# Prompt attention of a hybrid decoder step: heads in pairs, and block products in place of a running sum

## The chip, the cores and the metric

The kernel runs on one core of one Trainium2 chip. The metric is the time of one execution on the device in microseconds (us). The engines have short names in the profile: PE (matrix multiply) with its weight loads PEld, DVE (vector), ACT (activation), POOL (GpSimd) and SP (which feeds the DMA queues). PSUM, the memory that PE writes, is the tile `ps` of eight banks with 512 fp32 columns each.

## The reference

One step of a decoder trunk of four layers for 512 prompt tokens and 8 x 8 sample tokens, width 1024. Layer 1 mixes tokens by stick-breaking attention with 16 heads of 64. For the prompt, this is all that the change touches:

```
qkv = (u @ w_qkv).reshape(Bn, T, 3, N_HEADS, HEAD_DIM)
...
z = jnp.einsum('bqhd,bkhd->bhqk', q_blk, keys).astype(jnp.float32) * (HEAD_DIM ** -0.5)
z = z + bias.astype(jnp.float32)[None, :, None, None]
mask = k_pos[None, :] < q_pos[:, None]
log_stay = jnp.where(mask, jax.nn.log_sigmoid(-z), 0.0)
between = lax.cumsum(log_stay, axis=3, reverse=True) - log_stay
a = jnp.where(mask, jnp.exp(jax.nn.log_sigmoid(z) + between), 0.0)
return jnp.einsum('bhqk,bkhd->bqhd', a.astype(vals.dtype), vals)
```

So each key's weight needs the sum of softplus(z) over all later keys that the query may see. Softplus is computed as max(z, 0) + ln(1 + exp(-|z|)).

## The kernel before

Only the stage called `attention` matters here. It lies after the products with `w_qkv` and some transposes, and before the attention of the sample tokens, which starts when it has ended. Scores are held with keys on the 128 partitions and queries along the columns. One head has four **pieces**, one for each block of 128 keys, taken from the last block (`kb` = 3) to the first: the piece of block `kb` has `512 - 128 kb` columns, so the pieces of a head have 128, 256, 384 and 512 columns, 1280 together. There are 16 heads and 64 pieces. All of it is fp32.

For one piece the engines do this, each in its own loop, tied together by semaphores:

- PE, `scores` (L715): the product of keys and queries, over the 64 rows of that head, into one of four banks. It waits until `weights` of four pieces earlier has read that bank.
- DVE, `biased`: adds the head's bias into `ZB` (L1762), then takes |z| into `EX` (L1764). ACT, `soft`: exp (L1293) and ln (L1295) of `EX`. DVE, `softplus`: max and add into `SP` (L1773).
- POOL, `mask_sp`: zeroes the part of the diagonal block that no query may see (L2198), copies it into `SUM` (L2203) and adds the earlier pieces' sum to the rest (L2205).
- PE, `cumulate`: adds onto the scores the product of a negated triangle with `SP` (L723) and, but for a head's first piece, of negated ones with the previous `SUM` (L727). Two pieces behind `scores`.
- ACT, `weights`: exp with the bias, from the bank into `AT` (L1303). POOL, `mask_a`: zeroes the diagonal block of that (L2215).
- PE, `values` (L740), once in a head, after its four pieces: four products with `VT`, 64 output rows. DVE, `take` (L1779), once in two heads: copies the result out of its bank.

A fp32 matmul has two records in the trace, one for each of its two passes over the columns, each with a weight load; so 64 calls of `scores` are 128 records. No queue or planner orders the work: each engine works its own loop off in order. PE's is the following.

```
for k in range(4 * NH + 5):
    if k < 4 * NH:
        scores(k)
    if 2 <= k < 4 * NH + 2:
        cumulate(k - 2)
    if k % 4 == 0 and 8 <= k:
        values(k // 4 - 2)
```

## Time and profile before

| what | us |
|---|---|
| median of 3 runs (lowest, highest) | 3921.86 (3911.35, 3925.43) |
| the profiled execution, its own time | 3924.92 |
| its span, from the first to the last instruction | 3923.2 |
| prompt attention, from DVE's first read of scores to the last copy out of PSUM | 999 to 1213.1 |
| mean granted PE clock over the whole span | 0.932 of 2.4 GHz |

The trace's times count from the first instruction of the span. A granted clock of 1.00 is 2.4 GHz and 0.50 is 1.2 GHz; a number in between is a mean over a stretch with both. A record's duration holds the time that its result takes to arrive, so consecutive matmuls overlap in their records: what a matmul costs PE is the distance from its start to the next one's start.

### The profile page before, as it was taken

Reading aid. Unit: us, or ns where it says so; the run is one execution under the profiler, and the core shown is the slowest. Engines: PE = TensorE matmul, PEld = TensorE weight load, DVE = VectorE, ACT = ScalarE, POOL = GpSimd, SP = SyncE. Lnnn points to the kernel's source line nnn. Section 1 sums busy time; section 2 is a strip of 40 time slices with the busy share of each in tenths; the row PEclk is TensorE's granted clock in tenths of the full one; section 3 lists DMA queues with packets and bytes.
Section 4 is the critical chain, followed back from the end, with each engine's and each line's share of the span. In section 5 each row is a group of like instructions: output and inputs, shape, how many; then the busy total and the mean of one; then the engine's idle time right before and its main releaser. Section 6 shows DMA issues by size and latency. Waiting matters only on the chain.

```text
span 3923.2 us, 76827 instructions
## 1 busy us (share of the span) xinstructions
PE 3539.9 (90%) x33232; PEld 3231.5 (82%) x33232; DVE 1576.9 (40%) x2263; ACT 1298.6 (33%) x2088; POOL 410.5 (10%) x862
## 2 busy tenths in 40 slices
PE   5998999989788789999688789988999989999996
PEld 3997999979336579999578678867999979889996
DVE  1435443231451244442534654454444244354422
ACT  2223443222442234442333322323444222244422
POOL 1000000000452100000000432300000000000000
PEclk9999999999797599999888799989999999989998
DMA  4554223353102242224432100014222444222221
GB/s 158 151 153 152 80 81 107 94 172 92 49 1 86 87 132 86 80 83 118 138 92 61 39 17 15 20 42 132 86 80 83 118 145 114 79 59 81 83 79 46
DMA packets 450251, 350.04 MB, mean 89 GB/s; under 512 B 14652, under 2 KB 417100, under 8 KB 449596
## 3 DMA queue, kind: packets, MB, share of 16 engines
q1 hardware_dynamic: 439776, 308.58, 26.6%
q0 software_dynamic: 9616, 35.34, 2.8%
q8 instruction: 208, 3.41, 0.4%
q10 hardware_dynamic: 608, 2.36, 0.2%
q14 instruction: 43, 0.35, 0.0%
HBM read 333.44 MB, written 12.79 MB: 88 GB/s over the span
## 4 chain that ended last, share of the span: by engine, by line
PE 83%; DVE 8%; issue 3%; POOL 2%; ACT 2%; DMA 2%; POOLq 0%; DVEq 0%; ACTq 0%
PE ps L593 58%; PE ps L891 6%; PE ps L817 3%; PE ps L818 2%; PE ps L819 2%; PE ps L659 2%; DMA raw<-in_ada_w 1%; PE ps L688 1%; PE ps L740 1%; PE ps L778 1%; DVE XMf L1838 1%; PE ps L604 1%; DVE XMl L1842 1%; PE ps L770 1%; PE ps L723 1%
## 5 line engine op out<-in xcount | busy, mean ns | idle before, releaser
L1590 DVE TENSOR_TENSOR SL<-raw,SH 128x1024 fp32r<-128x1024 f32 x408 | 500.5, 1227 | 1544.4 <-ACT SH L1205 1544.4
L1205 ACT ACTIVATE SH<-raw 128x1024 fp32r<-128x1024 f32 x408 | 432.2, 1060 | 1596.3 <-PE ps L593 1358.4
L593 PE MATMUL ps<-Uh,SH 128*128 128x288 f32 x3744 | 806.1, 297 | 1.5 <-DVE GP L2069 1.1
L593 PE MATMUL ps<-Uh,SL 128*128 128x288 f32 x3744 | 801.7, 296 | 0.0
L593 PE MATMUL ps<-Ul,SH 128*128 128x288 f32 x3744 | 801.0, 296 | 0.0
L593 PEld LDWEIGHTS ps<-Uh,SH 128*128 128x128 f32 x3744 | 602.4, 189 | 18.4 <-issue 16.9
L593 PEld LDWEIGHTS ps<-Uh,SL 128*128 128x128 f32 x3744 | 603.3, 189 | 0.0
L593 PEld LDWEIGHTS ps<-Ul,SH 128*128 128x128 f32 x3744 | 603.3, 189 | 0.0
L593 PE MATMUL ps<-Hh,SH 128*128 128x288 f32 x1792 | 390.7, 300 | 2.4 <-DVE Hl L1829 2.4
L593 PE MATMUL ps<-Hh,SL 128*128 128x288 f32 x1792 | 383.9, 296 | 0.0
L593 PE MATMUL ps<-Hl,SH 128*128 128x288 f32 x1792 | 383.7, 296 | 0.0
L593 PEld LDWEIGHTS ps<-Hh,SH 128*128 128x128 f32 x1792 | 287.7, 189 | 13.1 <-issue 12.5
L593 PEld LDWEIGHTS ps<-Hh,SL 128*128 128x128 f32 x1792 | 288.9, 189 | 0.0
L593 PEld LDWEIGHTS ps<-Hl,SH 128*128 128x128 f32 x1792 | 288.9, 189 | 0.0
L2162 POOL COPY TL<-GP 128x2 f32 (+1 forms) x104 | 45.5, 438 | 1425.4 <-ACT GP L1205 1065.6
L817 PE MATMUL ps<-XMh,SH 128*128 128x288 f32 x448 | 141.5, 316 | 36.8 <-DVE XMl L1842 36.8
L659 PE MATMUL ps<-raw,CT 128*32 128x256 f32 x1408 | 120.3, 428 | 42.6 <-DMA raw<-in_ada_w 42.4
L1742 DVE SCALAR_TENSOR_TENSOR CV<-GP,ST,CV 128x592 f32<-128x592 f32 x176 | 147.0, 835 | 25.6 <-DVE CV L1742 0.6
L818 PE MATMUL ps<-XMl,SH 128*128 128x288 f32 x448 | 137.1, 306 | 0.0
L819 PE MATMUL ps<-XMh,SL 128*128 128x288 f32 x448 | 136.3, 304 | 0.0
L1205 ACT ACTIVATE Hh<-Hf (+1 forms) x112 | 76.0, 685 | 170.4 <-DVE Hf L2102 108.2
L817 PEld LDWEIGHTS ps<-XMh,SH 128*128 128x128 f32 x448 | 89.0, 199 | 45.8 <-issue 36.3
(407 smaller groups left out, 4854.3 us busy)
## 6 DMA issues: line engine op xcount, KB each, us to landing
raw<-in_ada_w SPq DMA_DIRECT2D x176, 512.0 KB, 4.3
raw<-in_f_w_gu SPq DMA_DIRECT2D x176, 512.0 KB, 3.8
raw<-in_f_w_down SPq DMA_DIRECT2D x64, 448.0 KB, 3.8
raw<-in_a_w_in SPq DMA_DIRECT2D x48, 512.0 KB, 5.1
raw<-in_f_w_down SPq DMA_DIRECT2D x32, 512.0 KB, 4.1
raw<-in_b_w_qkv SPq DMA_DIRECT2D x24, 512.0 KB, 4.6
raw<-in_r_w_rkv SPq DMA_DIRECT2D x24, 512.0 KB, 4.2
PRE<-in_ada_w SPq DMA_DIRECT2D x4, 2048.0 KB, 25.4
```

The costliest lines, as they stand in the source:

```text
L593: mm = pe.matmul(ps[:, b + h, 0:TH], w, a[:, k, h * TH:(h + 1) * TH], start=on, stop=off)
L604: mm = pe.matmul(ps[32 * g:32 * g + 32, SS, 0:TQ], ones[:], SQ[:, n % 2, g * TQ:(g + 1) * TQ], start=(k == 0), stop=(k == KT - 1), skip_gr ...
L659: mm = pe.matmul(ps[32 * g:32 * g + 32, ADA, 0:2 * P], CT[:, k, :], src[:, 2 * P * g:2 * P * g + 2 * P], start=(k == 0), stop=(k == KT - 1 ...
L688: mm = pe.transpose(ps[0:cols, bank, g * width:g * width + rows], a, ident[0:rows, 0:rows])
L817: pe.matmul(out, wh, hi[:, cols], start=start, stop=False)
L818: pe.matmul(out, wh, lo[:, cols], start=False, stop=False)
L819: return pe.matmul(out, wl, hi[:, cols], start=False, stop=stop)
L891: mm = lambda out, l, r, start=False: pe.matmul(out, l, r, start=start, stop=True, skip_group_check=True)
L1205: copy = lambda out, in_: act.activation(out, in_, ACT.Copy)
L1590: dve.tensor_tensor(SL[:, m.mod(2)], raw[:, n.mod(4)], SH[:, m.mod(2)].bitcast(F32), ALU.subtract)\
L1742: ins = dve.scalar_tensor_tensor(CV[:, 0:CW], src, w(tap), CV[:, 0:CW], ALU.mult, ALU.add)
L2162: pool.tensor_copy(tl[:, 0:HIST], GP[:, g, NP_TOK:NP_TOK + HIST])
```

## The change

- Heads are taken in pairs that lie in the two halves of the partitions. A piece is now both heads of a pair: 8 pairs, 32 pieces. DVE's, ACT's and POOL's instructions on `ZB`, `EX` and the masks cover both heads at once; `weights` stays one instruction for each head, with its own bias.
- `scores` issues the two heads' products one behind the other, the one on rows 0 to 63 and the other on rows 64 to 127, into two banks. There are three such pairs of banks in place of four single ones; the wait is for `weights` of three pieces earlier. `values` alternates between the heads, whose outputs are partitions 0 to 63 and 64 to 127 of one bank.
- `SUM`, its copy and its addition on POOL are gone. In their place `later_blocks` multiplies the negated ones with each of the earlier pieces' softplus tiles, which all stay in `SPS`: for the second, third and fourth piece 1, 2 and 3 products a head, with 128, 128 + 256 and 128 + 256 + 384 columns. It waits for `biased` of its own piece.
- The order on PE is `later_blocks(k)`, `scores(k + 2)`, `cumulate(k)`; `values` follows the first piece of the next pair. On POOL `mask_a(k - 1)` now stands ahead of `mask_sp(k)`. On ACT `weights` is two pieces behind `soft`, not three.

```
@@ -174,11 +174,22 @@
         KR = sb("KR", [P, 4, D], F32, u_at + 20 * D)
         KS = sb("KS", [NS_TOK, D], F32, h_at + 19 * S // 4)
         w1_at, w2_at, w3_at = u_at + 20 * D, h_at + 2 * S, h_at + 19 * S // 4
-        ZB = sb("ZB", [P, 2, 512], F32, w1_at)
-        EX = sb("EX", [P, 2, 512], F32, w1_at + 4096)
-        SP = sb("SP", [P, 2, 512], F32, w1_at + 8192)
-        SUM = sb("SUM", [P, 2, 512], F32, w1_at + 12288)
-        AT = sb("AT", [P, 2, 1280], F32, w2_at)
+        ZB = sb("ZB", [P, 2, 2, 512], F32, w1_at)
+        EX = sb("EX", [P, 2, 2, 512], F32, w1_at + 8192)
+        AT = sb("AT", [P, 2, 2, 1280], F32, h_at + 15 * S // 4)
+        SPS = [sb(f"SP{q}", [P, 2, 1280], F32, at) for q, at in enumerate((h_at + 15 * S // 4 + 20480, w2_at))]
+        PIECES = 4 * KT
+
+        def block_cols(pc):
+
+
+            return pc // 4, 3 - pc % 4, NP_TOK - (3 - pc % 4) * P, (0, P, 3 * P, 6 * P)[pc % 4]
+
+        def spent(pc):
+
+            p, kb, w, at = block_cols(pc)
+            return SPS[p % 2][:, :, at:at + w]
+
...
@@ -704,50 +715,56 @@
                 pe.wait_ge(tr_free, count["tr"])
 
 
-                def where(pc):
-                    return pc // 4, 3 - pc % 4
-
                 def scores(pc):
-                    h, kb = where(pc)
-                    r, w = 64 * (h % 2), NP_TOK - kb * P
-                    if due(pc - 3):
-                        pe.wait_ge(a_ready, pc - 3)
-                    pe.matmul(ps[:, pc % 4, 0:w], KF[r:r + HD, h // 2, kb * P:(kb + 1) * P],
-                              QF[r:r + HD, h // 2, kb * P:NP_TOK], start=True, stop=True).then_inc(z_ready, 1)
+                    p, kb, w, _ = block_cols(pc)
+                    if due(pc - 2):
+                        pe.wait_ge(a_ready, pc - 2)
+                    for h, hh in HEADS:
+                        mm = pe.matmul(ps[:, 2 * (pc % 3) + h, 0:w], KF[hh, p, kb * P:(kb + 1) * P], QF[hh, p, kb * P:NP_TOK],
+                                       start=True, stop=True)
+                    mm.then_inc(z_ready, 1)
 
                 def cumulate(pc):
 
-                    h, kb = where(pc)
-                    w = NP_TOK - kb * P
+                    p, kb, w, _ = block_cols(pc)
                     pe.wait_ge(spm_ready, pc + 1)
-                    mm = pe.matmul(ps[:, pc % 4, 0:w], ntri[:], SP[:, pc % 2, 0:w], start=False, stop=True,
-                                   skip_group_check=True)
-                    if kb < 3:
-                        pe.wait_ge(sum_ready, pc)
-                        mm = pe.matmul(ps[:, pc % 4, P:w], nones[:], SUM[:, (pc - 1) % 2, 0:w - P],
-                                       start=False, stop=True, skip_group_check=True)
+                    for h in range(2):
+                        mm = pe.matmul(ps[:, 2 * (pc % 3) + h, 0:w], ntri[:], spent(pc)[:, h], start=False, stop=True,
+                                       skip_group_check=True)
                     mm.then_inc(cum_done, 1)
 
-                def values(h):
-                    r, b = 64 * (h % 2), 4 + h // 2 % 2
-                    pe.wait_ge(am_ready, 4 * h + 4)
-                    if due(h // 2 - 1):
-                        pe.wait_ge(av_read, h // 2 - 1)
-                    at = AT[:, h % 2, :]
+                def later_blocks(pc):
+
+                    p, kb, w, _ = block_cols(pc)
+                    if kb == 3:
+                        return
+                    pe.wait_ge(zb_ready, pc + 1)
+                    for h in range(2):
+                        for later in range(3 - kb, 0, -1):
+                            pe.matmul(ps[:, 2 * (pc % 3) + h, later * P:w], nones[:], spent(pc - later)[:, h], start=False,
+                                      stop=True, skip_group_check=True)
+
+                def values(p):
+                    pe.wait_ge(am_ready, 4 * p + 4)
+                    if due(p - 1):
+                        pe.wait_ge(av_read, p - 1)
                     for kb in range(4):
-                        o0 = (0, P, 3 * P, 6 * P)[3 - kb]
-                        w = NP_TOK - kb * P
-                        mm = pe.matmul(ps[r:r + HD, b, kb * P:NP_TOK], VT[:, kb, h * HD:(h + 1) * HD],
-                                       at[:, o0:o0 + w], start=(kb == 0), stop=(kb == 3))
+                        _, _, w, at = block_cols(3 - kb)
+                        for h, hh in HEADS:
+                            mm = pe.matmul(ps[hh, 6 + p % 2, kb * P:NP_TOK], VT[:, kb, (2 * p + h) * HD:(2 * p + h + 1) * HD],
+                                           AT[:, p % 2, h, at:at + w], start=(kb == 0), stop=(kb == 3), skip_group_check=True)
                     mm.then_inc(av_done, 1)
 
-                for k in range(4 * NH + 5):
-                    if k < 4 * NH:
-                        scores(k)
-                    if 2 <= k < 4 * NH + 2:
-                        cumulate(k - 2)
-                    if k % 4 == 0 and 8 <= k:
-                        values(k // 4 - 2)
+                for k in range(2):
+                    scores(k)
+                for k in range(PIECES + 1):
+                    if k < PIECES:
+                        later_blocks(k)
+                        if k + 2 < PIECES:
+                            scores(k + 2)
+                        cumulate(k)
+                    if k % 4 == 0 and 4 <= k:
+                        values(k // 4 - 1)
 
 
                 pe.wait_ge(av_read, KT + 2)
@@ -1287,27 +1304,28 @@
 
                 def soft(pc):
 
-                    w = NP_TOK - (3 - pc % 4) * P
-                    e = EX[:, pc % 2, 0:w]
+                    _, _, w, _ = block_cols(pc)
+                    e = EX[:, pc % 2, :, 0:w]
                     act.wait_ge(abs_ready, pc + 1)
                     act.activation(e, e, ACT.Exp, scale=-1.0).then_inc(act_seq, 1)
                     act.wait_ge(act_seq, pc + 1)
                     act.activation(e, e, ACT.Ln, bias=1.0).then_inc(ln_ready, 1)
 
                 def weights(pc):
-                    h, kb = pc // 4, 3 - pc % 4
-                    w, o0 = NP_TOK - kb * P, (0, P, 3 * P, 6 * P)[3 - kb]
+                    p, _, w, at = block_cols(pc)
                     act.wait_ge(cum_done, pc + 1)
-                    if due(h - 1):
-                        act.wait_ge(av_done, h - 1)
-                    act.activation(AT[:, h % 2, o0:o0 + w], ps[:, pc % 4, 0:w], ACT.Exp, bias=BB[:, h:h + 1])\
-                       .then_inc(a_ready, 1)
+                    if due(p - 1):
+                        act.wait_ge(av_done, p - 1)
+                    for h in range(2):
+                        ins = act.activation(AT[:, p % 2, h, at:at + w], ps[:, 2 * (pc % 3) + h, 0:w], ACT.Exp,
+                                             bias=BB[:, 2 * p + h:2 * p + h + 1])
+                    ins.then_inc(a_ready, 1)
 
                 act.preload_act_table_set("natural_log_exp_and_others")
-                for k in range(4 * NH + 3):
-                    if k >= 3:
-                        weights(k - 3)
-                    if k < 4 * NH:
+                for k in range(PIECES + 2):
+                    if k >= 2:
+                        weights(k - 2)
+                    if k < PIECES:
                         soft(k)
 
                 for g in range(4 * NB):
@@ -1755,40 +1773,39 @@
                 dve.wait_ge(kv_out, 64)
 
                 def biased(pc):
-                    h, kb = pc // 4, 3 - pc % 4
-                    w = NP_TOK - kb * P
-                    z, e = ZB[:, pc % 2, 0:w], EX[:, pc % 2, 0:w]
+                    p, _, w, _ = block_cols(pc)
+                    z, e = ZB[:, pc % 2, :, 0:w], EX[:, pc % 2, :, 0:w]
                     dve.wait_ge(z_ready, pc + 1)
-                    dve.tensor_scalar(z, ps[:, pc % 4, 0:w], BB[:, h:h + 1], None, ALU.add).then_inc(zb_ready, 1)
+                    dve.tensor_tensor(z, ps[:, 2 * (pc % 3):2 * (pc % 3) + 2, 0:w],
+                                      BB[:, 2 * p:2 * p + 2].rearrange("p (h o) -> p h o", o=1).broadcast_to([P, 2, w]), ALU.add)\
+                       .then_inc(zb_ready, 1)
                     dve.wait_ge(zb_ready, pc + 1)
                     dve.scalar_tensor_tensor(e, z, -1.0, z, ALU.mult, ALU.max).then_inc(abs_ready, 1)
 
                 def softplus(pc):
-                    w = NP_TOK - (3 - pc % 4) * P
+                    p, _, w, _ = block_cols(pc)
                     dve.wait_ge(ln_ready, pc + 1)
-                    if due(pc - 1):
-                        dve.wait_ge(cum_done, pc - 1)
-                    if due(pc - 1):
-                        dve.wait_ge(sum_ready, pc - 1)
-                    dve.scalar_tensor_tensor(SP[:, pc % 2, 0:w], ZB[:, pc % 2, 0:w], 0.0, EX[:, pc % 2, 0:w],
+                    if due(p - 1):
+                        dve.wait_ge(cum_done, 4 * (p - 1))
+                    dve.scalar_tensor_tensor(spent(pc), ZB[:, pc % 2, :, 0:w], 0.0, EX[:, pc % 2, :, 0:w],
                                              ALU.max, ALU.add).then_inc(sp_ready, 1)
 
                 def take(p):
 
-                    dve.wait_ge(av_done, 2 * p + 2)
-                    dve.tensor_copy(Hf[:, p, 0:NP_TOK], ps[:, 4 + p % 2, :]).then_inc(av_read, 1)
-
-                for k in range(4 * NH + 10):
-                    if k < 4 * NH:
+                    dve.wait_ge(av_done, p + 1)
+                    dve.tensor_copy(Hf[:, p, 0:NP_TOK], ps[:, 6 + p % 2, :]).then_inc(av_read, 1)
+
+                for k in range(PIECES + 4):
+                    if k < PIECES:
                         if due(k - 1):
                             dve.wait_ge(sp_ready, k - 1)
                         biased(k)
-                    if 1 <= k < 4 * NH + 1:
+                    if 1 <= k < PIECES + 1:
                         softplus(k - 1)
-                    if k % 8 == 5 and k >= 13:
-                        take(k // 8 - 1)
-
-                dve.wait_ge(cum_done, 4 * NH)
+                    if k % 4 == 2 and 6 <= k:
+                        take(k // 4 - 1)
+
+                dve.wait_ge(cum_done, PIECES)
                 dve.memset(QB[:], 0.0).then_inc(av_read, 1)
                 dve.wait_ge(av_read, KT + 1)
                 dve.tensor_copy(QB[0:HD, :, 0, :], QF[0:HD, :, NP_TOK:T])
@@ -2190,36 +2207,25 @@
                     pool.dma_start(PG[:, n % 4, :], cache[0, bass.ds(page[n % (NB * NPAGE)], 1)]
                                    .rearrange("o t h d -> (o t) (h d)")).then_inc(page_full[n % 4], 16)
 
+                def diagonal(a):
+
+                    return pool.affine_select(out=a, in_=a, compare_op=ALU.is_gt, fill=0.0, base=0, pattern=[[0, 2], [1, P]],
+                                              channel_multiplier=-1)
+
                 def mask_sp(pc):
-                    h, kb = pc // 4, 3 - pc % 4
-                    w = NP_TOK - kb * P
                     pool.wait_ge(sp_ready, pc + 1)
-                    d = SP[:, pc % 2, 0:P]
-                    pool.affine_select(out=d, in_=d, compare_op=ALU.is_gt, fill=0.0, base=0, pattern=[[1, P]],
-                                       channel_multiplier=-1).then_inc(spm_ready, 1)
-                    pool.wait_ge(spm_ready, pc + 1)
-                    if due(pc):
-                        pool.wait_ge(cum_done, pc)
-                    ins = pool.tensor_copy(SUM[:, pc % 2, 0:P], d)
-                    if kb < 3:
-                        ins = pool.tensor_tensor(SUM[:, pc % 2, P:w], SUM[:, (pc - 1) % 2, 0:w - P],
-                                                 SP[:, pc % 2, P:w], ALU.add)
-                    ins.then_inc(sum_ready, 1)
-                    pool.wait_ge(sum_ready, pc + 1)
+                    diagonal(spent(pc)[:, :, 0:P]).then_inc(spm_ready, 1)
 
                 def mask_a(pc):
-                    h, kb = pc // 4, 3 - pc % 4
-                    o0 = (0, P, 3 * P, 6 * P)[3 - kb]
+                    p, _, _, at = block_cols(pc)
                     pool.wait_ge(a_ready, pc + 1)
-                    d = AT[:, h % 2, o0:o0 + P]
-                    pool.affine_select(out=d, in_=d, compare_op=ALU.is_gt, fill=0.0, base=0, pattern=[[1, P]],
-                                       channel_multiplier=-1).then_inc(am_ready, 1)
-
-                for k in range(4 * NH + 3):
-                    if k < 4 * NH:
+                    diagonal(AT[:, p % 2, :, at:at + P]).then_inc(am_ready, 1)
+
+                for k in range(PIECES + 1):
+                    if k >= 1:
+                        mask_a(k - 1)
+                    if k < PIECES:
                         mask_sp(k)
-                    if k >= 3:
-                        mask_a(k - 3)
 
                 def same_sequence(a):
 
```

## Rows read from the trace of the kernel before

**Rows 1.** The page: span, and the chain that ended last by engine.
```profile
span 3923.2 us, 76827 instructions
...
PE 83%; DVE 8%; issue 3%; POOL 2%; ACT 2%; DMA 2%; POOLq 0%; DVEq 0%; ACTq 0%
```

**Rows 2.** Stretches: busy us of PE, PEld, DVE, ACT, POOL, then clock, DMA.
```profile
999.00:1025.53 26.53, 21.07 (x37) 9.87 (x37) 13.07 (x26) 10.64 (x24) 9.40 (x24) 0.50 0.00 1
1088.79:1136.86 48.07, 39.82 (x120) 18.57 (x120) 25.75 (x50) 21.10 (x47) 26.36 (x61) 0.97 0.00 1
1136.86:1191.47 54.61, 45.63 (x121) 20.05 (x120) 25.74 (x50) 22.27 (x49) 25.96 (x60) 0.87 0.00 0
999.00:1213.10 214.10, 178.06 (x474) 80.65 (x474) 104.12 (x200) 87.31 (x192) 102.82 (x241) 0.86 0.00 1
```

**Rows 3.** Waits, 1100.7 to 1124.5: total us, times, longest.
```profile
ACT EX L1293 <- DVE EX L1764: 12.5, 6, 4.2
...
PEld ps L723 <- POOL SP L2198: 5.1, 4, 1.4
```

**Rows 4.** Timeline of one head: start, duration, engine, line.
```profile
1100.72 2.37 PE L740 MATMUL ps<-AT,VT 128*64 128x512 f32 x8 [0.73 <-POOL AT L2215]
...
1103.02 0.70 PE L715 MATMUL ps<-QF,KF 64*128 64x256 f32 x2
...
1103.64 1.12 PE L723 MATMUL ps<-SP,ntri 128*128 128x512 f32 x2
...
1104.61 0.81 PE L727 MATMUL ps<-SUM,nones 128*128 128x384 f32 x2
...
1105.35 0.91 PE L715 MATMUL ps<-QF,KF 64*128 64x384 f32 x2
...
1112.65 2.37 PE L740 MATMUL ps<-AT,VT 128*64 128x512 f32 x8 [0.73 <-POOL AT L2215]
```

**Rows 5.** Timeline: first mask, and last copy out of PSUM.
```profile
1003.71 0.28 POOL L2198 TENSOR_SCALAR_AFFINE_SELECT SP<-SP 128x128 f32<-128x128 f32 x1 [11.80 <-issue]
...
1212.39 0.69 DVE L1779 COPY Hf<-ps 128x512 f32<-128x512 f32 x1 [7.82 <-PE ps L740]
```

**Rows 6.** Timeline of PE in a later layer, at 2297.6.
```profile
2297.59 1.91 PE L891 MATMUL ps<-BMs,UWs 64*64 64x512 f32 x8
2299.31 1.05 PE L891 MATMUL ps<-KMs,TMs 64*64 64x512 f32 x4
```

**Rows 7.** Timeline of PE in the transposes.
```profile
987.20 1.15 PE L688 MATMUL ps<-ident,KF 128*128 128x128 f32 x8 [0.19 <-ACT KR L1205]
```

**Rows 8.** Groups of lines, 999 to 1213.1: busy us, mean ns, idle before.
```profile
L2205 POOL TENSOR_TENSOR SUM<-SUM,SP 128x128 f32<-128x128 f32 (+2 forms) x48 | 41.3, 859 | 0.1
...
L1764 DVE SCALAR_TENSOR_TENSOR EX<-ZB 128x128 f32<-128x128 f32 (+1 forms) x64 | 34.5, 538 | 2.2
L1773 DVE SCALAR_TENSOR_TENSOR SP<-ZB,EX 128x128 f32<-128x128 f32 (+1 forms) x64 | 33.8, 529 | 1.8 <-ACT EX L1295 0.8
L1303 ACT ACTIVATE AT<-ps,BB 128x128 f32<-128x128 f32 (+1 forms) x64 | 33.0, 515 | 15.0 <-PE ps L727 11.8 <-PE ps L723 1.9
...
L1293 ACT ACTIVATE EX<-EX 128x128 f32<-128x128 f32 (+1 forms) x64 | 29.9, 467 | 113.6 <-DVE EX L1764 113.6
L2215 POOL TENSOR_SCALAR_AFFINE_SELECT AT<-AT 128x128 f32<-128x128 f32 x64 | 24.6, 386 | 6.9 <-ACT AT L1303 2.5
...
L2203 POOL COPY SUM<-SP 128x128 f32<-128x128 f32 x64 | 20.4, 318 | 10.1 <-PE ps L727 7.1 <-PE ps L723 0.3
...
L2198 POOL TENSOR_SCALAR_AFFINE_SELECT SP<-SP 128x128 f32<-128x128 f32 x64 | 18.9, 295 | 98.1 <-DVE SP L1773 86.2 <-issue 11.8
```

**Rows 9.** Groups by shape, sample tokens' attention, 1298 to 1325.
```profile
L1818 DVE SCALAR_TENSOR_TENSOR SZ<-SZ,SE 128x1024 f32<-128x1024 f32 x2 | 4.1, 2084 | 0.0
...
L2227 POOL TENSOR_SCALAR_AFFINE_SELECT SE<-SE 64x1024 f32<-64x1024 f32 x1 | 2.0, 2022 | 6.2 <-ACT SE L1329 6.2
...
L1818 DVE SCALAR_TENSOR_TENSOR SZ<-SZ,SE 64x1024 f32<-64x1024 f32 x1 | 1.2, 1209 | 0.0
```

More of the change, by code:

```diff
@@ L311, in trunk_program @@
         dve_seq, pool_seq, act_seq = sem("dve_seq"), sem("pool_seq"), sem("act_seq")
-        (z_ready, zb_ready, abs_ready, ln_ready, sp_ready, spm_ready, sum_ready, cum_done, a_ready, am_ready,
+        (z_ready, zb_ready, abs_ready, ln_ready, sp_ready, spm_ready, cum_done, a_ready, am_ready,
          av_done, av_read) = (sem(f"at_{n}") for n in
-                              ("z_ready", "zb_ready", "abs_ready", "ln_ready", "sp_ready", "spm_ready", "sum_ready",
+                              ("z_ready", "zb_ready", "abs_ready", "ln_ready", "sp_ready", "spm_ready",
                                "cum_done", "a_ready", "am_ready", "av_done", "av_read"))
@@ L1323, in attention @@
                     act.activation(e, e, ACT.Exp, scale=-1.0).then_inc(act_seq, 1)
-                    act.wait_ge(act_seq, 4 * NH + n + 1)
+                    act.wait_ge(act_seq, PIECES + n + 1)
                     act.activation(e, e, ACT.Ln, bias=1.0).then_inc(sln, 1)
@@ L2232, in same_sequence @@
                                               pattern=[[0, NH], [NT, NB], [1, NT]], channel_multiplier=-1)
-                pool.wait_ge(av_done, NH)
+                pool.wait_ge(av_done, KT)
                 pool.wait_ge(kv_out, 64)
```

## The prediction

> **What bounds the kernel now.** I read the page first. It gives the span of 3923.2 us and a chain that runs through PE for 83% of it [rows 1], but that is a mean over stages; the change touches one stage only, so the question is what ends last inside prompt attention. Next came the stretches [rows 2]: the stage is 214.1 us long, 5.5% of the span. Its DMA share is 0.00, so no transfer is part of the argument. No engine is full: in 48.07 us PE's records cover 39.8, DVE's 25.8, POOL's 26.4, ACT's 21.1. The clock matters: 0.50 for the first 26.5 us, 0.97 in the second stretch, 0.87 in the third, and the last two hold four heads each (48.07 against 54.61 us).
>
> Then the timeline of one head at the full clock [rows 4]. The period is 1112.65 - 1100.72 = 11.93 us. The four products of `values` have 1280 columns and take 1103.02 - 1100.72 = 2.30 us; 1280 columns at 4 cycles of 2.4 GHz, 1.667 ns each, are 2.13. So a column costs 1.667 ns, and a switch between forms 0.17: the score product of 256 columns takes 0.62 (0.43 + 0.19), the triangle of 512 takes 0.97 (0.85 + 0.12), `SUM`'s of 384 takes 0.74 (0.64 + 0.10). A head has 1280 columns of scores, 1280 of triangle, 768 of `SUM` and 1280 of values: 4608 columns, 7.68 us. So 4.25 of the 11.93 us are no streaming: switches and waits. The waits tell which [rows 3]: in two heads the triangle's weight load waits 5.1 us for POOL's mask, and ACT waits 12.5 us for DVE, which waits for scores that stand on PE behind the stalled product. The loop PE, DVE, ACT, DVE, POOL, PE is what sets the period, with PE's 64% streaming inside it.
>
> **The change, part by part**, for one pair (two heads, 23.86 us before at full clock).
>
> *PE's columns.* Triangle: 2560 as before, 4.27 us. The ones' products: 1280 a head in place of 768, so 2560, 4.27 us; that is +1024 columns, +1.71 us a pair.
>
> *Side by side.* Scores and values have 2560 columns each, 4.27 us each if they run one after the other. The nearest row is another layer's, with two heads in opposite halves of rows and of output partitions [rows 6]: eight records, four matmuls of 512 columns, start 1.72 us ahead of the next group, where 2048 columns at 1.667 ns are 3.41. Disjoint parts of PE do overlap, twofold in a long row of them. Each matmul is two passes, and if starts stay in order, the first head's second pass overlaps the second head's first: n matmuls take n + 1 passes in place of 2n. I take 3/4 for the two of `scores` (3.2 us a pair) and 9/16 for the eight of `values` (2.4). The ends are 1/2 and 1.
>
> *Switches.* `scores` now comes 4 times a pair, not 8. I charge 0.35 us each for going in and out, and 0.11 for a start after a stall.
>
> *Weight loads.* The added products are short, 128 columns the most often. Eight fp32 matmul records of 128 columns with a 128-wide weight each take 1.15 us with the last one's tail [rows 7]; a pass over 128 columns is 0.107 us and eight are 0.85, so the loads hide behind the passes, and I add nothing. The Trainium skill says otherwise: its page "TensorE: Matmul & The Clock Gate", Part 3, has weight loads overlap running matmuls only where they use other rows of the array. By that rule six more full-height matmuls a pair, two loads each of some 0.107 us (an estimate from the same page, 128 columns at 1.2 GHz), would add 1.3 us a pair, 11 us in all. The trace does not bear it out, since eight passes and eight such loads in a row would need 1.7 us.
>
> *DVE, ACT.* Instructions halve in number and double in length. `EX` and `SP` cost 34.5 and 33.8 us over the stage [rows 8]. An uncontended instruction of 1024 elements costs 1.209 [rows 9], about 0.155 + 1.04 ns an element, so a pair's four cost 3.3 us each way, and `biased` much the same; with the 0.69 of `take` [rows 5], DVE has some 10.7 us of work a pair. ACT: `soft` 3.0 for each of its two (29.9 / 8 now [rows 8], less four starts of 0.2), `weights` 8 instructions x 0.515 [rows 8] = 4.1, together 10.1. Neither fills the period.
>
> *POOL.* 41.3 + 20.4 us of addition and copy go [rows 8]. A mask now has 256 elements, not 128 at 0.295; 1024 elements took 2.02 us [rows 9], 1.97 ns each, so some 0.55. But a collision shows: DVE's instruction of 1024 elements with two inputs from SBUF takes 2.084 us while POOL masks, 1.209 alone [rows 9], and `mask_a` already averages 0.386 against 0.295 for `mask_sp` [rows 8]. I take 0.65 for `mask_sp`, 0.75 for `mask_a` and 12% more for `EX` and `SP`; bounds are 0.55 and nothing, and 0.85, 0.95 and 50%.
>
> *The new order.* `scores(k + 2)` waits for `weights(k - 1)`, so that the next product cannot start before; `cumulate(k)` and `values` stand behind it. On POOL `mask_sp(k)` stands behind `mask_a(k - 1)`, which waits for the same `weights`: both masks, 1.1 us, now lie between one product's `weights` and the next product. The handoffs are some 0.06 us, 0.3 from a last column to its reader (0.17 of tail [rows 4] and an estimate for the rest). I lay the period out without collision, from the start of the first piece's triangle:
>
> - 0.0: first triangle. Then values 0.4 to 3.2, the ones of the second piece to 3.6, scores of the fourth to 5.2.
> - 5.2: second triangle, 0.85. PE was the limit up to here. The third piece's ones to 7.4, the next pair's first scores to 8.0. But DVE got the fourth piece's scores at 5.5, needs 2.4 us for bias and |z|, and only then makes the third piece's softplus (to 8.9); after its mask:
> - 9.6: third triangle, to 11.0; the fourth piece's ones, twice 128 + 256 + 384 columns, 2.56 us, to 13.6; scores to 14.6.
> - 14.6: fourth triangle, to 16.3; its `weights` to 17.9; scores of the next pair's third piece, to 19.4. Next pair.
>
> With the collisions 19.8 us, against 23.86: 4.0 us a pair. PE has 14.1 us of passes in it, 71%.
>
> **The sum.** The first mask starts at 1003.71, after POOL's own preparation [rows 5], which stays. The first triangle starts at 1004.4. The first pair runs at the low clock, as two heads did [rows 2]: laid out again with 3.33 ns a column up to 1027, where the low level ends if it lasts as long as before, it takes 26.2 us. Six pairs at 19.8 are 118.9, to 1149.5. The last pair, up to its copy out of PSUM, takes 22.6: 1172.1. The clock's later dips cost the third stretch 54.61 - 48.07 = 6.5 us [rows 2]; I put 6 for them: 1178. Before the last copy ends at 1212.39 + 0.69 = 1213.08 [rows 5]. The gain is 35 us, 0.9%. What follows, the loads of cached pages and the sample tokens, starts on this end and moves with it whole. The profiled execution took 3924.92 us, 1.7 more than its span and 3.1 over the median; it becomes 3890, and the median 3921.86 becomes 3887.
>
> **The rivals.**
>
> *Halves don't overlap* for K = 64 and 512 columns across two banks, or for 64 output columns at 128 rows: no row has just these forms. Scores cost 1.07 more a pair and values 1.9: period 22.6, end 1194.8 and 6 for dips: 12 us gained, 3910. Against it stands [rows 6].
>
> *The hand-over of masks.* With POOL and DVE at the upper bounds (0.85, 0.95, 50%) the period is 21.4, the end 1184.2 + 6 = 1190: 23 us gained, 3899. For it: both masks are in the loop now. Against: the longest overlaps were POOL's long additions, which go.
>
> *The clock.* This one ends on the other side. The stage began at 0.50 and stayed there for 26.5 us though PE's records covered 21 of them [rows 2], and it dipped later. If side by side work or the waits keep the clock at 0.50 for all pairs, a pair takes 31.8 and the stage ends at 1257, 44 us later: 3966. Each pair at the low level costs 12 us beyond 1164 (all but no low level at all), so four pairs of eight eat the gain and six make it slower by over 0.5%. Against it: the share of passes rises from 64% to 71% in time, 86% in columns, and by the layout no pause of PE is longer than 1.8 us (0.73 now where [rows 4] show one). The Trainium skill's page "TensorE: Matmul & The Clock Gate", Part 1, lets activity release the clock and idleness take it back; by that the denser loop should be no colder. The sum doesn't use it.
>
> *The ones' products eat it.* By the skill's rule on weight loads above, 11 us less gain, 3898; I give it no more than 1 in 20, for [rows 7].
>
> **How the numbers follow.** The forecast as laid out 0.62; masks' hand-over or weight loads 0.13; halves not overlapping 0.12; the clock low for four pairs 0.07, for six or more 0.06. The forecast's own low end is full overlap (19.3 a pair, 1167.2), no later dip, no collisions (3.4 us) and a low level that ends 8 us sooner (2.4): 1161.4, 52 us gained, 3870, and 3866 with the scatter of the runs. The high end takes in the halves that don't overlap: 3912. Runs of before spread over 14 us, and 0.5%, 20 us, is about what this measurement can tell from no change. Faster by over 0.5%, below 3902: the forecast, masks and a little of the rest, 0.77. Within: 0.17. Slower: 0.06.
>
> **What would show it.** In the profile after: `values`, every fourth piece, some 19.8 us apart at full clock; two products of scores of 512 columns in about 1.3 us (1.7 would be the rival) and eight of `values` in 2.4 to 2.8; the ones' six products of the fourth piece in 2.6 (3.8 by the skill's rule); masks of 0.55 to 0.75; third triangle waiting on POOL; the copy of the last pair ending near 1178; the sample tokens' part unchanged and only earlier. I am wrong if `scores` waits long for `weights`, if the granted clock stays near 0.5 past 1031, or if DVE's long instructions stretch by half.

## The result, and the profile after

The median went from 3919.89 to 3858.65 us, a ratio of 0.9836 (95% interval 0.9815 to 0.9856): 61 us, where 35 were forecast and 3866 was the low end of the range. (The kernel before has one run more here than in the table further up, so its median is 3919.89.) In the profiled executions, one of each kernel, the span fell by 65.7 us, and all of it lies in prompt attention: the last copy out of PSUM ends at 1147.09, not at 1213.08 [rows 5], 66.0 us sooner, while what follows takes 2710.4 us against 2710.1. The page of the changed kernel begins with its span:

```profile
span 3857.5 us, 76448 instructions
```

Busy time by stretch, the same view as [rows 2] (after the stretch: its length, the busy time of PE, PEld, DVE, ACT, POOL, then the clock):

```profile
999.00:1020.00 21.00, 15.17 (x56) 9.26 (x56) 10.93 (x15) 10.38 (x19) 3.73 (x9) 0.75 0.00 1
1020.00:1147.10 127.10, 106.07 (x512) 59.83 (x508) 73.27 (x87) 64.89 (x110) 29.13 (x56) 1.00 0.00 1
999.00:1147.10 148.10, 121.24 (x564) 69.09 (x564) 84.21 (x102) 75.28 (x128) 32.85 (x64) 0.96 0.00 1
```

The clock is 1.00 from 1020 on and 0.96 over the stage, where it was 0.86. The timeline of one pair, to be laid beside [rows 4]:

```profile
1059.63 1.13 PE L723 MATMUL ps<-QF,KF 64*128 64x512 f32 x4
...
1061.65 1.47 PE L744 MATMUL ps<-SP,nones 128*128 128x128 f32 x8
...
1063.28 1.16 DVE L1790 SCALAR_TENSOR_TENSOR SP<-ZB,EX 128x768 f32<-128x768 f32 x1
...
1064.50 0.41 POOL L2212 TENSOR_SCALAR_AFFINE_SELECT SP<-SP 128x256 f32<-128x256 f32 x1 [0.88 <-DVE SP L1790]
...
1064.96 1.56 PE L732 MATMUL ps<-SP,ntri 128*128 128x384 f32 x4 [1.41 <-POOL SP L2212]
...
1066.36 2.76 PE L744 MATMUL ps<-SP,nones 128*128 128x128 f32 x12
...
1069.05 0.70 PE L723 MATMUL ps<-QF,KF 64*128 64x256 f32 x4
...
1073.02 0.92 PE L723 MATMUL ps<-QF,KF 64*128 64x384 f32 x4 [1.35 <-ACT AT L1320]
...
1073.87 0.71 PE L732 MATMUL ps<-SP,ntri 128*128 128x128 f32 x4
...
1074.51 2.37 PE L754 MATMUL ps<-AT,VT 128*64 128x512 f32 x16
...
1076.81 0.71 PE L744 MATMUL ps<-SP,nones 128*128 128x128 f32 x4
```

Three things are to be seen. First, the four records of the score products of 512 columns (both heads) cost 1060.69 - 1059.63 = 1.06 us with the switch, 0.21 more than one head's columns alone (0.85), and sixteen records of `values`, two heads, cost 1076.81 - 1074.51 = 2.30, exactly what one head's eight did in [rows 4]. The halves run fully side by side. Second, the ones' twelve records of a fourth piece take 1069.05 - 1066.36 = 2.69 for 2.56 us of columns: their weight loads are hidden. Third, what waits are left: 1.41 us for the third piece's mask, which comes straight behind its softplus (1063.28 to 1064.44), and 1.35 for `weights` to give a bank back. Two of the waits of [rows 3] and two new ones, 1056.7 to 1092.3, which is two pairs, so four heads, where [rows 3] cover two:

```profile
ACT AT L1320 <- PE ps L732: 13.5, 8, 3.3
PEld ps L723 <- ACT AT L1320: 5.0, 4, 2.2
PEld ps L732 <- POOL SP L2212: 4.3, 4, 1.6
...
ACT EX L1310 <- DVE EX L1783: 3.0, 4, 0.8
```

ACT's 12.5 us of waiting for DVE in two heads have become 3.0 in four; in their place it waits 13.5 us in four heads for PE's triangle. The ends of the stage, for the sums below:

```profile
1003.24 1.22 PE L732 MATMUL ps<-SP,ntri 128*128 128x128 f32 x4 [12.46 <-POOL SP L2212]
...
1020.38 0.71 PE L732 MATMUL ps<-SP,ntri 128*128 128x128 f32 x4
...
1127.35 0.71 PE L732 MATMUL ps<-SP,ntri 128*128 128x128 f32 x4
...
1146.40 0.69 DVE L1796 COPY Hf<-ps 128x512 f32<-128x512 f32 x1 [8.30 <-PE ps L754]
```

So the first pair took 17.14 us, each of the next six 17.83, and the last 19.74 with its copy. The groups that answer to [rows 8]:

```profile
L744 PE MATMUL ps<-SP,nones 128*128 128x128 f32 (+2 forms) x192 | 40.2, 353 | 0.0
...
L1790 DVE SCALAR_TENSOR_TENSOR SP<-ZB,EX 128x256 f32<-128x256 f32 (+3 forms) x32 | 29.1, 910 | 2.5 <-ACT EX L1312 2.4
...
L1783 DVE SCALAR_TENSOR_TENSOR EX<-ZB 128x256 f32<-128x256 f32 (+3 forms) x32 | 26.4, 825 | 1.1
...
L2212 POOL TENSOR_SCALAR_AFFINE_SELECT AT<-AT 128x256 f32<-128x256 f32 x32 | 20.5, 639 | 98.0 <-ACT AT L1320 98.0
...
L2212 POOL TENSOR_SCALAR_AFFINE_SELECT SP<-SP 128x256 f32<-128x256 f32 x32 | 13.2, 412 | 22.3 <-issue 11.8 <-DVE SP L1790 10.4
```

### The profile page after: what moved, and what is told of

The parts are those of the page before. It is cut to its first block, busy times and chain, and to the rows that moved or that the text cites. A ratio compares the mean times of both kernels' runs of the same rounds, so it can differ in the third digit from the quotient of the medians.

```text
span 3857.5 us, 76448 instructions
## 1 busy us (share of the span) xinstructions
PE 3480.1 (90%) x33328; PEld 3218.1 (83%) x33328; DVE 1558.1 (40%) x2167; ACT 1286.8 (33%) x2024; POOL 340.4 (9%) x686
## 4 chain that ended last, share of the span: by engine, by line
PE 84%; DVE 8%; DMA 2%; ACT 2%; issue 2%; POOL 1%; POOLq 0%; DVEq 0%; ACTq 0%
PE ps L604 59%; PE ps L908 6%; PE ps L834 3%; PE ps L836 2%; PE ps L835 2%; PE ps L670 2%; DMA raw<-in_ada_w 2%; PE ps L699 1%; PE ps L795 1%; DVE XMf L1855 1%; PE ps L732 1%; PE ps L615 1%; DVE XMl L1859 1%; PE ps L787 1%; PE ps L627 1%
## 5 line engine op out<-in xcount | busy, mean ns | idle before, releaser
L604 PEld LDWEIGHTS ps<-Hh,SH 128*128 128x128 f32 x1792 | 288.1, 189 | 13.1 <-issue 12.5
```

The lines of the kernel that those rows point to most:

```text
L604: mm = pe.matmul(ps[:, b + h, 0:TH], w, a[:, k, h * TH:(h + 1) * TH], start=on, stop=off)
```

## The experiments

All were compared with the kernel before, each round with runs of its own: the median of the kernel before was 3924.23, 3919.57 and 3923.07 us in the three rounds. The ratios are those of that comparison, not quotients of the medians shown. The end of the stage (last copy out of PSUM) is the sharper reading, since the runs of one kernel scatter by up to 26 us while nothing but the stage is changed; but it comes from one profiled execution of each kernel. A period is the distance from one pair's `values` to the next pair's.

| kernel | median us, ratio to before (95%) | stage ends at | period of a pair at clock 1.00 |
|---|---|---|---|
| before | 3919.89 | 1213.08 | 23.86 |
| changed | 3858.65, 0.9836 (0.9815 to 0.9856) | 1147.09 | 17.83 |
| values_in_turn | 3864.82, 0.9847 (0.9831 to 0.9864) | 1161.73 | 19.38 |
| scores_parted | 3888.83, 0.9909 (0.9892 to 0.9925) | 1179.80 | 21.25 |
| both_parted | 3912.27, 0.9983 (0.9970 to 0.9997) | 1204.27 | none without a dip |
| blocks_one_head | 3895.52, 0.9919 (0.9902 to 0.9936) | 1189.38 | 22.16 |
| blocks_after_mask | 3884.47, 0.9907 (0.9881 to 0.9932) | 1172.56 | 19.95 |
| one_ahead | 3979.27, 1.0150 (1.0124 to 1.0176) | 1270.87 | none without a dip |
| before_warm | 3913.48, 0.9982 (0.9966 to 0.9998) | 1201.63 | 23.84 |
| before_filled | 3904.70, 0.9965 (0.9951 to 0.9979) | 1193.97 | 23.87 |
| after_warm | 3857.18, 0.9839 (0.9819 to 0.9859) | 1146.30 | 17.83 |
| mask_sp_first | 3856.26, 0.9826 (0.9794 to 0.9858) | 1144.53 | 17.62 |
| softplus_first | 3854.49, 0.9830 (0.9802 to 0.9859) | 1146.45 | 17.43 |
| three_edits | 3844.92, 0.9815 (0.9796 to 0.9834) | 1135.06 | 16.35 |

**values_in_turn.** The changed kernel, `values` head by head:

```
-for kb in range(4):
-    for h, hh in HEADS:
+for h, hh in HEADS:
+    for kb in range(4):
```

> The changed kernel with the products of values in another order: all four of a pair's first head, then all four of the second, so that neighbours use the same half of PE. Theory (the two halves ran fully side by side, and values stands where PE is the limit): values takes 4.3 us in place of 2.30, the period of a pair rises from 17.83 to 19.7 to 20.0, the stage ends 15 to 17 us later than in the changed kernel. Rival (the hand-over between DVE, ACT and POOL sets the period and hides what PE saves): period below 18.4, under 5 us in all.

```profile
1081.39 3.93 PE L754 MATMUL ps<-AT,VT 128*64 128x512 f32 x16
...
1100.78 3.93 PE L754 MATMUL ps<-AT,VT 128*64 128x512 f32 x16
```

A pair's sixteen records are 3.93 us, not 2.37; 1.55 us a pair and 14.6 in all are lost. The size is a little under the theory's, since the second head's first record starts 1.56 us after the first head's, beside that head's last two products. The rival (under 5 us) falls by the trace: `values` stands on the path, and every period is 19.38 at a clock of 1.00. The medians show less of it: 6 us against the changed kernel's, and only 2 when each is set against its own round's kernel before (59.4 us gained, not 61.2). The profiled execution, 3878.25 us, is the longest of its four.

**scores_parted.** A full-height product of two columns between the heads' scores:

```
 for h, hh in HEADS:
+    if h:
+        pe.matmul(ps[:, 2 * (pc % 3) + h, 0:2], ntri[:], ident[:, 0:2], start=True, stop=True,
+                  skip_group_check=True)
     mm = pe.matmul(ps[:, 2 * (pc % 3) + h, 0:w], KF...
```

> The changed kernel with a full-height product of 2 columns between the two heads' scores, into columns that the second score product overwrites, so that they cannot run side by side. Theory: scores takes 4.3 us a pair in place of 2.1, and the extra product about 0.4 each time, 3.7 us more on PE of which 2.5 to 3.5 show in the period (17.83 to 20.3 to 21.3): the stage ends 20 to 28 us later. Rival (scores runs in pauses anyway): period up by less than 1 us.

```profile
1096.90 1.12 PE L726 MATMUL ps<-QF,KF 64*128 64x512 f32 x2
1097.96 0.38 PE L724 MATMUL ps<-ident,ntri 128*128 128x2 f32 x2
1098.27 1.12 PE L726 MATMUL ps<-QF,KF 64*128 64x512 f32 x2
1099.32 1.13 PE L735 MATMUL ps<-SP,ntri 128*128 128x256 f32 x4
```

The period rises by 3.42 us, at the top of the theory's range, and the stage ends 32.7 us later, beyond it. The 3.42 us are not the overlap's alone. The scores of 512 columns now take 1099.32 - 1096.90 = 2.42 us where they took 1.06, 1.36 more: 0.85 are the lost overlap, and 0.5 are the extra product with its switches. Over the four pieces that is 2.1 us of lost overlap and 2.0 of extra work a pair, of which 3.42 show; so between 1.4 and 2.1 of them are the overlap's. The rest of the 32.7 us came from a clock that dipped, though PE's records cover more of the time than in the changed kernel:

```profile
1000.00:1050.00 50.00, 42.94 (x150) 24.36 (x152) 21.76 (x28) 20.07 (x35) 8.16 (x17) 0.83 0.00 1
1050.00:1100.00 50.00, 45.92 (x189) 25.11 (x186) 24.68 (x31) 21.06 (x36) 9.65 (x18) 0.97 0.00 0
1100.00:1150.00 50.00, 45.25 (x186) 26.07 (x185) 26.57 (x32) 22.52 (x38) 9.27 (x18) 0.97 0.00 1
```

**both_parted.** The two diffs above at once.

> The changed kernel with both undoings at once: values head by head, and the 2-column product between the scores of the two heads. What stays of the change is the pairs' longer instructions, the block products and the order. Theory (the two add up: 14.6 and 32.7 us later one by one): the last copy ends near 1194, period 22.8 at the full clock. Rival (both fill the same pause): near 1183.

It ends at 1204.27, 10 us beyond the sum of the two, with the clock below 1.00 throughout (0.83 to 0.99 in pieces of 20 us from 1020 to 1180). The rival, that both fill one pause, falls. The kernel without side by side work is thus 57 us behind the changed one and 9 ahead of the kernel before. The 57 us are more than side by side work is worth: up to 16 of them (2.0 a pair) are the extra products, and a part that no run separates is the low clock.

**blocks_one_head.** The kernel before, with one part of the change: block products in place of `SUM`, heads one at a time.

```
+for later in range(3 - kb, 0, -1):
+    pe.matmul(ps[:, pc % 4, later * P:w], nones[:], spent(pc - later), start=False, stop=True,
+              skip_group_check=True)
 pe.wait_ge(spm_ready, pc + 1)
 mm = pe.matmul(ps[:, pc % 4, 0:w], ntri[:], spent(pc), ...)
-if kb < 3:
-    pe.wait_ge(sum_ready, pc)
-    mm = pe.matmul(ps[:, pc % 4, P:w], nones[:], SUM[:, (pc - 1) % 2, 0:w - P], ...)
...
-ins = pool.tensor_copy(SUM[:, pc % 2, 0:P], d)
```

> The kernel before with one part of the change alone: no running sum on POOL, products with the ones for each earlier piece in its place, heads still one at a time. Theory (side by side work, instructions of twice the length and fewer of them make the gain): a head has 512 more columns, 0.85 us, and loses POOL's additions and copies, so the period stays at 11.9 to 12.8 us; total within 15 us of before. Rival (the running sum on POOL was the bound): 10.8 us a head or less, 18 us or more gained.

```profile
1102.84 2.37 PE L743 MATMUL ps<-AT,VT 128*64 128x512 f32 x8
...
1113.92 2.37 PE L743 MATMUL ps<-AT,VT 128*64 128x512 f32 x8
```

The theory was wrong and the rival nearer: 11.08 us a head in place of 11.93, 23.7 us sooner. PE has 0.85 us more work a head and the loop is faster. POOL's additions no longer stand before the next mask: in two heads the triangle's weight load waits 1.5 us for POOL's mask, where it waited 5.1 [rows 3]:

```profile
PEld ps L731 <- POOL SPB L2199: 1.5, 4, 0.4
```

DVE's `EX` of 512 columns also takes 0.69 us where it averaged 0.84; no run separates the two. 13.6 of the 23.7 us are the period's. The rest goes with the clock, which was 1.00 in every stretch from 1020 on; it ran without the later dips, and no idle product was needed for that.

**blocks_after_mask.** The ones' products behind the next scores and the mask's wait:

```
-later_blocks(k)
 if k + 2 < PIECES:
     scores(k + 2)
+pe.wait_ge(spm_ready, k + 1)
+later_blocks(k)
 cumulate(k)
```

> The changed kernel with the products for later blocks behind the wait for the mask and behind the next scores, as in the kernel before. Theory (PE fills its waits with them): the 1.3 and 2.6 us of ones' products of the third and fourth piece no longer lie in a wait, the period rises from 17.83 to 20.3 to 21.5, the stage ends 20 to 28 us later. Rival (PE has pauses enough anyway): period up by less than 1 us.

The period is 19.95, 2.12 us longer, just under the theory's range; the stage ends 25.5 us later, with two periods that hold a dip of the clock. The rival falls.

**one_ahead.** Scores one piece ahead:

```
 later_blocks(k)
-if k + 2 < PIECES:
-    scores(k + 2)
+if k + 1 < PIECES:
+    scores(k + 1)
```

> The changed kernel with scores one piece ahead of the sums, not two. Theory (a piece's way through DVE, ACT, DVE and POOL is 4 to 6.5 us and a step of PE about 4.5, so it is hidden only in part): period 18.5 to 20, the stage 5 to 17 us later. Rival, two pieces ahead is what the gain comes from: period 21.5 or more, 30 us or more later.

It ends 124 us later, 58 behind the kernel before: far outside the theory's 5 to 17 us, and within what the rival allowed. A part of it, which no run separates, is the clock's, 0.76 on average over the stage. My theory named the right loop and missed an order: on DVE the softplus of piece k stands behind the bias of piece k + 1, which needs the scores that PE issues just ahead of the triangle of piece k. So scores, bias, magnitude, softplus, mask and triangle follow each other in every step:

```profile
1180.41 1.47 PE L744 MATMUL ps<-SP,nones 128*128 128x128 f32 x8
...
1181.81 1.13 PE L723 MATMUL ps<-QF,KF 64*128 64x512 f32 x4
1183.06 1.22 DVE L1778 TENSOR_TENSOR ZB<-ps,BB 128x1024 f32<-128x1024 f32 x1 [3.54 <-PE ps L723]
1184.32 1.23 DVE L1782 SCALAR_TENSOR_TENSOR EX<-ZB 128x1024 f32<-128x1024 f32 x1
1185.46 0.95 DVE L1789 SCALAR_TENSOR_TENSOR SP<-ZB,EX 128x768 f32<-128x768 f32 x1
...
1186.48 0.41 POOL L2211 TENSOR_SCALAR_AFFINE_SELECT SP<-SP 128x256 f32<-128x256 f32 x1 [4.56 <-DVE SP L1789]
...
1186.94 2.14 PE L732 MATMUL ps<-SP,ntri 128*128 128x384 f32 x4 [4.00 <-POOL SP L2211]
```

Behind its scores PE waits 4.00 us for a chain that begins with its own scores; the three triangles before this one waited 2.55 to 3.20 us for their masks. With two pieces ahead that chain spans two steps.

**before_warm, before_filled.** Idle products into an unused bank in the kernel before: 13 of 512 columns during the first wait, and for before_filled also in each head ahead of three waits:

```
+if k == 2:
+    for _ in range(13):
+        pe.matmul(ps[:, 7, :], ntri[:], QF[:, 0, 0:512], start=True, stop=True, skip_group_check=True)
...
+if pc % 4 in (1, 2):
+    n = P * (pc % 4)
+    pe.matmul(ps[:, 7, 0:n], ntri[:], QF[:, 0, 0:n], start=True, stop=True, skip_group_check=True)
```

> The kernel before with 13 extra full products of 512 columns into an unused bank while PE waits for the first mask, nothing else changed. Theory (the low clock at the start comes from PE's pause ahead of the stage): the clock stays at 1.00 through the first heads, the first values starts near 1016 in place of 1025.5, the stage ends 8 to 12 us sooner, later dips as before. Rival (the loop of the kernel before is itself too sparse for the full clock): the clock falls again within the first heads and less than 3 us are gained.

> The kernel before with the 13 warming products of before_warm and, in every head, idle products of 128, 256 and 128 columns into an unused bank right ahead of the waits for a mask (0.60 and 0.91 us) and of values (0.73). Theory (the low clock in the last third comes from how sparse PE's work is; the changed kernel is rid of it because it is denser): clock 1.00 in all heads, the last copy ends near 1195, 6 to 7 us sooner than in before_warm, so 18 of the 66 us are the clock's. Rival (the dips belong to the moment or to the chip): the dips stay and the stage ends at 1201 or later.

Both ends of the stage came out as the theories had them: 11.5 us sooner with the first alone, 7.7 more with the second. The first `values` of before_warm started at 1019.15, not 1016, for the clock dipped once in between (0.57 from 1016 to 1020), and the later dip stayed: eight records of `values` took 4.06 us or more, against 2.37 at the full clock, in heads 11 to 14, where it was 10 to 14. The same stretches as in [rows 2], before_filled:

```profile
999.00:1027.00 28.00, 25.55 (x80) 12.28 (x79) 16.84 (x33) 13.59 (x31) 13.04 (x33) 1.00 0.00 1
1088.79:1136.86 48.07, 44.14 (x146) 22.16 (x145) 26.04 (x51) 22.08 (x51) 26.52 (x62) 1.00 0.00 1
1136.86:1191.47 54.61, 48.97 (x163) 24.55 (x162) 25.97 (x49) 23.04 (x51) 29.73 (x69) 1.00 0.00 1
```

The period is what it was, 11.93 a head. So the idle products hide in waits and change nothing but the clock: the low level cost the kernel before 19.1 us. The medians of the same round agree, 3923.07 against 3904.70, 18.4 us.

**after_warm.** The like in the changed kernel, before the first triangle:

```
+if k == 0:
+    for _ in range(12):
+        pe.matmul(ps[:, 7, :], ntri[:], QF[:, 0, 0:512], start=True, stop=True, skip_group_check=True)
 cumulate(k)
```

> The changed kernel with 12 full products of 512 columns into an unused bank while PE waits for the first mask. Theory (only the 6 us up to 1009 ran at the low clock there): first values 2 to 4 us sooner, the stage ends 2 to 4 us sooner. Rival (the extra products keep the first triangle back): no gain or a loss.

0.8 us sooner, less than expected. From its first triangle to the second pair's the first pair took 15.68 us, not 17.14, so the low clock up to about 1009 cost the changed kernel 1.5 us; but the first triangle began 0.64 later. That the first pair is no slower than the rest even at the low clock comes from what it lacks: no `values` stand in it, 2.30 us in every later pair.

**mask_sp_first.** The two masks on POOL in the other order:

```
+if k < PIECES:
+    mask_sp(k)
 if k >= 1:
     mask_a(k - 1)
-if k < PIECES:
-    mask_sp(k)
```

> The changed kernel with the softplus mask of piece k ahead of the weights mask of piece k - 1 on POOL, so that the product no longer stands behind both. Theory now (the mask is ready before PE has finished the scores, or comes straight from a late softplus): period within 0.2 us of 17.83, the stage within 2 us. Rival, the hand-over of masks as the prediction had it: 0.4 us for each piece, 1.6 a pair, 13 us sooner.

2.6 us sooner and a period 0.21 shorter, just beyond the theory's bounds and far from the rival's 1.6; the masks' hand-over, one of the prediction's terms, was little of what the loop waited for.

**softplus_first.** On DVE softplus ahead of the next piece's bias:

```
+if 1 <= k < PIECES + 1:
+    softplus(k - 1)
 if k < PIECES:
     if due(k - 1):
         dve.wait_ge(sp_ready, k - 1)
     biased(k)
-if 1 <= k < PIECES + 1:
-    softplus(k - 1)
```

> The changed kernel with softplus of piece k - 1 ahead of bias and magnitude of piece k on DVE. Theory (the third piece's triangle waits 1.4 us because its softplus stands on DVE behind the fourth piece's bias, which waited for its scores): the wait goes, period 16.4 to 17.0, the stage ends 7 to 11 us sooner. Rival (DVE then waits for ACT's ln with the next bias behind it): period 18.0 or more.

```profile
1062.21 0.96 DVE L1790 SCALAR_TENSOR_TENSOR SP<-ZB,EX 128x768 f32<-128x768 f32 x1 [1.05 <-ACT EX L1312]
...
1064.49 1.39 POOL L2212 TENSOR_SCALAR_AFFINE_SELECT SP<-SP 128x256 f32<-128x256 f32 x1
...
1065.93 1.56 PE L732 MATMUL ps<-SP,ntri 128*128 128x384 f32 x4 [1.01 <-POOL SP L2212]
```

The period fell by 0.4 us, but the first pair took 2 us longer, and the stage ended 0.6 sooner; neither side's numbers fit. Softplus was ready earlier, at 1063.17, but its mask stood on POOL behind the other mask until 1064.49 and then took 1.39 us beside DVE's long instructions. The triangle still waited 1.01 us.

**three_edits.** The last three diffs together.

> The changed kernel with after_warm's products, mask_sp_first's order on POOL and softplus_first's on DVE. Theory: the gains add up (0.6, 2.6 and 2 to 4 us), the last copy ends between 1139 and 1142, period 17.2 to 17.4. Rival (softplus_first's first pair took 2 us longer and its waits stand in the same places): 1143 or later.

```profile
1051.20 2.37 PE L754 MATMUL ps<-AT,VT 128*64 128x512 f32 x16
...
1055.21 0.96 DVE L1793 SCALAR_TENSOR_TENSOR SP<-ZB,EX 128x768 f32<-128x768 f32 x1 [0.90 <-ACT EX L1315]
...
1056.24 0.41 POOL L2215 TENSOR_SCALAR_AFFINE_SELECT SP<-SP 128x256 f32<-128x256 f32 x1 [3.83 <-DVE SP L1793]
...
1057.58 0.49 PE L723 MATMUL ps<-QF,KF 64*128 64x128 f32 x4
...
1058.00 1.56 PE L732 MATMUL ps<-SP,ntri 128*128 128x384 f32 x4
...
1067.56 0.65 PE L754 MATMUL ps<-AT,VT 128*64 128x512 f32 x2
```

More than the sum, and below the theory's range: 16.35 us a pair, 12.0 us sooner than the changed kernel. With its own queue free the third piece's mask follows softplus at once, and the triangle (1058.00) starts as soon as PE has issued the scores; the wait of 1.41 us is gone. 3844.92 us is the best time here. In the same comparison after_warm ran at 3849.69 to 3857.68 and this at 3842.22 to 3848.61.

## Why the prediction was wrong in size

The mechanism and the layout held: the loop through all engines, who waits for whom, PE as the limit in the second piece's step, the third triangle late by DVE's order. What failed are sizes of terms, nearly all to one side. The stage was forecast to end at 1178, at best at 1161.4, and ended at 1147.1. The 31 us are 1.2 of an earlier first triangle, 9.1 in the first pair, 11.9 in the next six, 2.9 in the last and 6 of dips.

- *The clock, in The sum.* "The first pair runs at the low clock, as two heads did", 26.2 us, was 17.14: 9.1 us. The "6 for them", the later dips, was 0. Not all of the 9.1 is the clock's, for the period's terms below are in it too. But the low level, taken to last to 1027 as before, ended near 1009 and cost only 1.5 us of the pair (after_warm). It ended between 1006 and 1016 in all kernels with pairs that were not warmed, near 1019 in blocks_one_head and at 1028 in the kernel before, each seen in one execution; no run shows why. The later dips hung on the loop: they are gone in before_filled and in blocks_one_head. The clock was listed only as a small help to the low end (8.4 us), and is up to half of the miss.
- *Side by side and switches.* "3/4 for the two of `scores` and 9/16 for the eight of `values`" was 1/2 and 1/2, the end of the bounds that the nearest row showed and that I left for a rule of my own about the order of passes. The switches, 0.35 a time, were near 0.2. On the path of one pair, `values` and the scores of 512, 256 and 384 columns measured 2.30, 1.06, 0.63 and 0.85 us, where the layout has 2.8, 1.6, 1.0 and 1.5: some 2 us less. The low end was mis-added too: it gave full overlap 0.5 us a pair, where the layout's own steps have 1.2 of those passes on the path.
- *Short products* went the other way: the first triangle and the second piece's ones, 0.4 each in the layout, took 0.64 each.
- *Collisions.* "0.65 for `mask_sp`, 0.75 for `mask_a` and 12%" were 0.412, 0.639, and 0 for `EX` (0.825 on average, what 640 elements cost alone) and 11% for `SP`. The uncontended mask took 0.41, not 0.55: 1.97 ns an element came from an instruction of four times the length. The 0.4 us a pair that were put on collisions do not show in the period.
- Together these bring the period from 19.8 to 17.83. From one triangle to the next the four steps measured 4.65, 4.27, 4.72 and 4.19 us, where the layout had 5.2, 4.4, 5.0 and 4.8 before collisions.
- *Weight loads* at nothing was right. By the rule that the Trainium skill gives on its page "TensorE: Matmul & The Clock Gate", Part 3, the fourth piece's ones would have taken some 3.8 us, an estimate with the prediction's 0.107 us a load; they took 2.69, so the measurement decides against it.
- *The rivals.* Halves that don't overlap: fallen. Masks: fallen as a bound. The clock: right that it could move the time by tens of us, wrong in direction. The Trainium skill's page "TensorE: Matmul & The Clock Gate", Part 1, has activity release the clock and idleness take it back. The first half agrees with before_warm and before_filled; scores_parted and both_parted do not bear the rule out, for their clock dipped with no pause of PE over 1.4 us between 1020 and 1150.

Where the 66.0 us are: 19.1 are the low clock of the kernel before, less 0.8 of the changed kernel's own (shown by before_filled and after_warm), and the 47.7 left are the period; 6.03 us for each of eight pairs would be 48.2. Of the 6.03, undoing the overlap of `values` costs 1.55, undoing that of `scores` 1.4 to 2.1 (3.42 with the extra product), and the block products alone bring 1.70. That leaves some 0.7 to 1.4 us for what no run takes apart: the pairs' longer and fewer instructions on DVE, ACT and POOL, and the new order, of which only the place of the ones' products was tried by itself (2.12 us, blocks_after_mask). The parts need not simply add up.

What stays open is why the clock dipped in scores_parted and both_parted although PE's records filled 87% and 88% of the stage, against 82% in the changed kernel. Nor does a filled PE divide the kernels: before_filled and blocks_one_head, at 91% and 93%, had no later dip, and one_ahead, at 63%, had the lowest clock of all. No run separates the share of rows in use from the order of the work.

## What to carry to other kernels

Find the loop that goes through all engines and lay its period out step by step; then ask for each in-order queue what stands ahead of the instruction that the loop needs. Swapping one order moved little until the order on the next queue was swapped too. And look at the granted clock of a latency-bound stage before forecasting it: a denser loop may get a higher one (blocks_one_head) or not (both_parted), and idle products in the waits tell how much that is worth.

## What the runs showed of the hardware

- Two fp32 products of 512 columns on opposite 64-row halves into two banks cost PE 1.06 us with the switch, and those of 64 output columns each (128 rows) into one bank cost two heads the time of one, 2.30 us. No extra pass is lost at the start.
- A POOL mask of 2 x 128 elements takes 0.41 us, and up to 1.39 beside DVE's instructions with two SBUF inputs.
- Full-height products of 128 to 384 columns, each pass with a new weight load, run at the rate of their columns: twelve records in 2.69 us, for 2.56 us of columns.
- Besides its start, the clock of the kernel before fell to the lower level in `values` of 5 of 16 heads, and in before_warm in 4 of the same 5; with idle products of 128 and 256 columns ahead of waits of 0.6 to 0.9 us added it stayed at 1.00 over the whole stage (before_filled).
